# Half B's keys are transposed by DMA, and a chunk's decay weight sits on its values alone

## The chip, the cores and the metric

The kernel runs on all 8 cores of one Trainium2 chip. Each core computes one of the 8 prompt sequences and 16 of the 128 sample tokens; nothing passes between cores. The metric is device time in microseconds of the slowest core, as a median over runs.

## The reference, cut to what matters

Two layers, of which the second is a retention layer; each is followed by a SwiGLU block. Retention goes chunk by chunk (128 tokens), with a decay gamma per head:

```python
def ret_chunk(q, k, v, s0, log_g):
    scores = jnp.einsum('bihd,bjhd->bhij', q, k) * dmask          # dmask[i,j] = gamma^(i-j), i >= j
    o = jnp.einsum('bhij,bjhe->bihe', scores, v)
    o = o + jnp.einsum('bihd,bhde->bihe', q, s0) * cross          # cross[i] = gamma^(i+1)
    s_new = gamma^c * s0 + jnp.einsum('bjhd,bjhe->bhde', k * kdec, v)   # kdec[j] = gamma^(c-1-j)
# per head: o is normalised over its 512 values (GroupNorm), then silu(g) * on, then @ w_out
```

There are 4 heads with 256 key and 512 value channels. The sample group does one such step per token from a given state of 4 x 256 x 512 per sample, read from and written back to HBM.

## The kernel before

A sequence of 2048 tokens is worked as two halves, A (hA, with the 16 meta and 16 sample tokens) and B (hB). The order is: pooling and feed-forward of layer 0 for A, retention of A, then the feed-forward of A and the feed-forward of B, beside which the sample group's states stream through, then retention of B (`ret(1, ...)`), then the last feed-forward of B.

The program is recorded op by op. `Prog` finds the dependences and `Side` plans the order: generators such as `a_gen` and `b_gen` run beside the main line, and each `yield` hands a delay or an operation, whose planned end (`_clock`, line 159, a table of costs) says when the generator is resumed. Thus the order on each engine is fixed when the program is built, by planned times; on the chip each engine goes through its own queue in that order and waits on semaphores.

In retention, per head h: `qk_proj` makes keys K and queries q (rotated by DVE and POOL); `a_gen` makes for each chunk t the masked scores PMt (two matmuls into a bank, a DVE multiply by the causal mask) and, through a second PSUM bank, the transposed keys KD[:, t] (two TensorE transposes, `tr`, line 488, and a ScalarE copy). `v_proj` makes V with a decay weight per token (C_VS). `b_gen` then does for each chunk PMt x V, q x state copy (Sbf), and adds KD x V to the running state in psS; ScalarE copies psS to Sbf for the next chunk. `gate_gen` normalises (C_GE is its epsilon) and gates the output; `o_proj` follows one head behind. Everything in psS is kept relative to a decay reference: before, each chunk's key copy is scaled by gamma^(-128 t) and each state copy by gamma^(128 (t+1)).

There are five or six PSUM banks for all this (`ring['b']`); `room(k)` waits in the plan until k of them are not held. KD and PMt have one buffer for all heads, so chunk t of head h waits for chunk t of head h - 1 to be used (`prog['b', h - 1]`).

DMAs go by two queues, each in order: SP's (`load` and `store`, line 520: states, outputs) and POOL's (weights). A DMA's waits stand on the issuing queue, so what follows on that queue waits too.

The lines that matter below: 481 `mm`, 489 `tr`, 498 `act`, 502 `acopy`, 505 `tt`, 514 `stto` (the sample group's state update on DVE), 202 the DMA issue.

## Time and profile before

| | us |
|---|---|
| median of 3 runs (1679.96 to 2389.19) | 1682.67 |
| the profiled execution, device time | 1678.12 |
| its span on the slowest core (core 3) | 1676.6 |
| spans of the cores | 1658.4 to 1676.6 |

| engine, slowest core | busy us | share of the span |
|---|---|---|
| PE (TensorE matmul) | 1606.3 | 96% |
| DVE | 756.1 | 45% |
| ACT | 689.9 | 41% |
| POOL | 337.2 | 20% |

The span runs from the first to the last instruction; the device time of the execution has 1.5 us around it. A busy PE is not a PE at its peak: matmuls overlap, so what one costs is read from the distance of starts, not from its duration. PEclk is the clock that TensorE was granted, 1.00 for 2.4 GHz and 0.50 for 1.2 GHz. On core 3 the stages lie as follows: start and layer 0 of A to about 335 us, retention of A to 620, sample group beside the feed-forward of A and B to 1155, retention of B to 1430, last feed-forward to 1676.

### The profile page before, as it was taken

To read this page: it belongs to the slowest core of one execution; us is meant where nothing else is said; L and a number is where in the kernel's file an instruction comes from. 1 tells how busy PE (TensorE), PEld (TensorE's weight loads), DVE (VectorE), ACT (ScalarE), POOL (GpSimd) and SP (SyncE) were. 2 spreads that over 40 slices of the span, in tenths; PEclk is the share of its full clock that TensorE was granted. 3 is DMA by queue.
4 is the path that set the end of the run, shared out by engine and by line. 5 is a ranking of instruction groups with operands and counts; after the bars stand their busy time and mean duration, and the time that the engine had idled before them with its cause. 6 is when DMAs were issued, how large, how long until landed. Compare 5 with 4: busy or idle time off the path is not lost.

```text
span 1676.6 us, 28802 instructions; the slowest of 8 cores (1658.4 to 1676.6 us)
## 1 busy us (share of the span) xinstructions
PE 1606.3 (96%) x10076; PEld 920.0 (55%) x10076; DVE 756.1 (45%) x1455; ACT 689.9 (41%) x1279; POOL 337.2 (20%) x560
## 2 busy tenths in 40 slices
PE   5999999999999999997999988999999998999997
PEld 3666666655555564443454433456545555666665
DVE  4432222643736563452363623355546648323225
ACT  3311012257555635545544414444565566110122
POOL 5110000343524311110010000013514232001000
PEclk9899999999999999998999999999999999999998
DMA  9157966787776788799988998676434313213433
GB/s 235 25 114 164 181 138 129 130 143 145 154 134 119 155 225 251 228 246 232 213 191 247 238 246 274 225 192 136 90 78 81 59 39 107 66 48 102 68 53 103
DMA packets 78892, 251.68 MB, mean 150 GB/s; under 512 B 8896, under 2 KB 15360, under 8 KB 78736
## 3 DMA queue, kind: packets, MB, share of 16 engines
q0 software_dynamic: 32656, 114.57, 38.3%
q1 hardware_dynamic: 46096, 135.27, 26.3%
q8 instruction: 85, 1.39, 0.3%
q14 instruction: 55, 0.45, 0.1%
HBM read 254.79 MB, written 73.27 MB: 196 GB/s over the span
## 4 chain that ended last, share of the span: by engine, by line
PE 82%; DMA 9%; DVE 3%; issue 2%; ACT 1%; SPq 1%; POOL 1%; DVEq 0%; POOLq 0%; ACTq 0%
PE pm L481 69%; PE psU L481 6%; DMA nrs<-fb 5%; PE psS L481 5%; DMA fb<-sret 2%; DMA nrs<-cs_sb 2%; PE pm L489 1%; SPq L202 1%; DVE xn L514 1%; DMA fb<-xtok 1%; PE pm L485 0%; DVE hB L505 0%; ACT on L498 0%; DVE stt L979 0%; DVE fb L514 0%
## 5 line engine op out<-in xcount | busy, mean ns | idle before, releaser
L481 PE MATMUL pm<-xn,w 128*128 128x512 bf16 (+7 forms) x4424 | 794.2, 338 | 13.3 <-DVE hB L505 5.7
L481 PEld LDWEIGHTS pm<-xn,w 128*128 128x128 bf16 x4424 | 432.6, 99 | 341.1 <-issue 33.4
L481 PE MATMUL pm<-U,w 128*128 128x512 bf16 (+6 forms) x2290 | 405.8, 334 | 3.7 <-DVE hA L505 2.6
L481 PEld LDWEIGHTS pm<-U,w 128*128 128x128 bf16 x2290 | 222.0, 98 | 168.3 <-issue 13.3
L505 DVE TENSOR_TENSOR U<-pm,rot 128x512 bf16<-128x512 f32 (+5 forms) x206 | 121.2, 588 | 367.7 <-PE pm L481 356.2
L498 ACT ACTIVATE rot<-pm 128x512 bf16<-128x512 f32 (+6 forms) x190 | 98.7, 519 | 370.5 <-PE pm L481 370.4
L505 DVE TENSOR_TENSOR hB<-pm,hB 128x347 f32<-128x347 f32 (+4 forms) x164 | 85.0, 539 | 86.7 <-PE pm L481 85.6
L481 PE MATMUL pm<-w,xn 128*128 128x512 bf16 (+1 forms) x488 | 113.3, 379 | 1.7 <-DVE U L505 1.7
L505 DVE TENSOR_TENSOR hA<-pm,hA 128x512 f32<-128x512 f32 (+4 forms) x131 | 76.0, 597 | 73.8 <-PE pm L481 73.2
L505 POOL TENSOR_TENSOR U<-rot 128x352 bf16<-128x352 f32 (+2 forms) x96 | 95.4, 1014 | 55.8 <-DVE rot L505 55.7
L498 ACT ACTIVATE af<-pm,cf_sb 128x128 f32<-128x128 bf16 x232 | 87.2, 462 | 24.0 <-DVE U L505 15.2
L505 DVE TENSOR_TENSOR rot<-pm,cs_sb 128x352 f32<-128x352 f32 (+2 forms) x168 | 78.5, 512 | 26.9 <-PE pm L481 14.3
L665 POOL TENSOR_TENSOR stt<-stt,cf_sb 128x1 f32<-128x1 f32 x65 | 36.3, 558 | 233.5 <-DVE stt L509 233.4
L498 ACT ACTIVATE Sbf<-psS 128x1024 bf16<-128x1024 f32 x56 | 57.4, 1025 | 56.1 <-PE psS L481 55.9
L498 ACT ACTIVATE U<-pm 128x256 bf16<-128x256 bf16 (+7 forms) x127 | 54.8, 451 | 60.3 <-PE pm L481 59.8
L481 PEld LDWEIGHTS pm<-w,xn 128*128 128x128 bf16 (+1 forms) x488 | 45.8, 98 | 54.3 <-issue 4.8
L498 ACT ACTIVATE U<-pm,cf_sb 128x512 bf16<-128x512 f32 (+1 forms) x77 | 52.6, 690 | 52.3 <-PE pm L481 52.0
L514 DVE SCALAR_TENSOR_TENSOR fb<-fb,psS 128x1024 f32<-128x1024 f32 x41 | 49.8, 1214 | 46.1 <-DMA fb<-sret 28.3
L202 POOL DMA_DIRECT2D w<-c_gu x49 | 27.6, 565 | 200.9 <-PE pm L481 197.9
L505 DVE TENSOR_TENSOR U<-af,U 128x512 bf16<-128x512 f32 x64 | 55.4, 866 | 23.2 <-ACT af L498 23.2
L498 ACT ACTIVATE xn<-hB 128x347 bf16<-128x347 f32 (+4 forms) x68 | 33.4, 508 | 59.9 <-DVE hB L505 59.5
L505 DVE TENSOR_TENSOR U<-pm,cb_sb 128x128 bf16<-128x128 f32 x54 | 15.6, 291 | 91.6 <-PE pm L489 70.9
(254 smaller groups left out, 1509.3 us busy)
## 6 DMA issues: line engine op xcount, KB each, us to landing
w<-c_gu POOLq DMA_DIRECT2D x49, 512.0 KB, 7.7
fb<-sret SPq DMA_DIRECT2D x41, 512.0 KB, 8.5
nrs<-fb SPq DMA_DIRECT2D x41, 512.0 KB, 8.4
w<-w_gu POOLq DMA_DIRECT2D x39, 512.0 KB, 9.3
w<-w_d POOLq DMA_DIRECT2D x32, 352.0 KB, 6.1
w<-c_d POOLq DMA_DIRECT2D x32, 352.0 KB, 5.1
c_gu<-w SPq DMA_DIRECT2D x17, 512.0 KB, 7.9
w<-w_qk POOLq DMA_DIRECT2D x16, 512.0 KB, 9.7
```

The source lines that it names most:

```text
L202: h.dma_start(out=o_ap, in_=i_ap).then_inc(s, 16)
L481: return P.op('pe', lambda h: h.matmul(out, lhsT=lhsT, rhs=rhs, start=start, stop=stop, skip_group_check=skip), ins=[lhsT, rhs], outs=[out ...
L489: return P.op('pe', lambda h: h.transpose(out, in_, idn), ins=[in_, idn], outs=[out], cost=0.056)
L498: return P.op('act', lambda h: h.activation(out=out, in_=in_, func=func, scale=scale, **kw), ins=ins, outs=[out] + ([accum] if accum is no ...
L505: return P.op(eng, lambda h: h.tensor_tensor(out=out, in0=a, in1=b, op=op), ins=[a, b], outs=[out])
L514: return P.op('dve', lambda h: h.scalar_tensor_tensor(out=out, in0=a, scalar=s, in1=b, op0=op0, op1=op1), ins=ins, outs=[out])
L665: return P.op('pool', lambda h: h.tensor_tensor(out=dst, in0=dst, in1=cf[0:n, C_NH:C_NH + k], op=ALU.pow), ins=[dst, cf[0:n, C_NH:C_NH + k ...
```

## The change

In half B the keys are transposed by 16 DMAs on SP's queue (`dma_start_transpose`, SBUF to SBUF, four chunks and one half of the key channels each, at t = 0 and t = 4 of every head) in place of 64 TensorE transposes, their bank and 32 ScalarE copies. For t = 0 and 4 the generator waits in the plan until four chunks of the previous head are used. Since a DMA cannot scale, the decay of the chunk goes into the values' weights: C_VS and C_GE get a column for each chunk, and in both halves the copies to KD and Sbf carry no scale. `b_gen` asks for 3 free banks in place of 4 and yields once more, `yield kdt[h, t]`, which in half B holds the transposing DMA and in half A None.

```diff
+        def xpose_dma(out, in_, sem):
+            return P.dma('sp', [(out, in_)], ins=[in_], outs=[out], sem=sem, transpose=True)
...
             for t in range(8):
-                while h and prog['b', h - 1] < t + 1:
-                    yield 0.3
+                if hf == 0:
+                    while h and prog['b', h - 1] < t + 1:
+                        yield 0.3
+                elif t % 4 == 0:
+                    while h and prog['b', h - 1] < t + 4:
+                        yield 0.3
+                    for c in range(2):
+                        xt = xpose_dma(KD[:, t:t + 4, c * 128:(c + 1) * 128], K[:, c, t * 128:t * 128 + 512], ('tk', c, t))
...
-                pt = bank()
-                ptb = pt[:].bitcast(BF16)[:, 0:256]
-                for c in range(2):
-                    tr(ptb[:, c * 128:(c + 1) * 128], K[:, c, cc], ident)
+                if hf == 0:
+                    pt = bank()
+                    ptb = pt[:].bitcast(BF16)[:, 0:256]
+                    for c in range(2):
+                        tr(ptb[:, c * 128:(c + 1) * 128], K[:, c, cc], ident)
                 tt(PMt[:, t, :], ps[:, 0:128], causal, ALU.mult)
                 held.remove(ps)
-                act(KD[:, t, :], ptb, ACT.Copy, scale=float(gam[h] ** (-128.0 * t)))
+                if hf == 0:
+                    acopy(KD[:, t, :], ptb)
                 prog['a', h] = t + 1
+                kdt[h, t] = xt if hf else None
...
-                yield from room(4)
+                yield kdt[h, t]
+                yield from room(3)
...
-                    xs = act(Sbf[(t + 1) % 2][:], psS[:], ACT.Copy, scale=float(gam[h] ** (128.0 * (t + 1))))
+                    xs = acopy(Sbf[(t + 1) % 2][:], psS[:])
...
-                sc = C_V8 if t == 8 else C_VS
-                act(V[0:n, t, :], pb[0:n, :], ACT.Copy, scale=cf[0:n, sc + h:sc + h + 1])
+                sc = (C_V8 if t == 8 else C_VS + 4 * t) + h
+                act(V[0:n, t, :], pb[0:n, :], ACT.Copy, scale=cf[0:n, sc:sc + 1])
...
-        cf[:, C_VS + h] = np.exp(-(j + 1.0) * lg[h])
+        for t in range(8):
+            cf[:, C_VS + 4 * t + h] = np.exp(-(128.0 * t + j + 1.0) * lg[h])
+            cf[:, C_GE + 4 * t + h] = EPS * 256.0 * np.exp(-2.0 * (128.0 * t + j + 1.0) * lg[h])
```

What stands on TensorE's queue at the start of head 0's value projection in half B (L481 `pm<-w,xn` is a value tile, `pm<-U` 128x128 a score, L489 `cb_sb,U` the key transposes, then the first chunk of `b_gen`), before:

```order
L481 MATMUL pm<-w,xn 128x512 x8
L481 MATMUL pm<-U 128x128 x2
L489 MATMUL pm<-cb_sb,U 128x128 x2
L481 MATMUL pm<-w,xn 128x512 x8
L481 MATMUL pm<-U 128x128 x2
L489 MATMUL pm<-cb_sb,U 128x128 x2
L481 MATMUL pm<-w,xn 128x512 x8
L481 MATMUL pm<-U 128x128 x2
L489 MATMUL pm<-cb_sb,U 128x128 x2
L481 MATMUL pm<-U 128x512
L481 MATMUL pm<-Sbf,U 128x512 x2
L481 MATMUL psS<-U 128x512 x2
```

and of the change, at the same place:

```order
L481 MATMUL pm<-w,xn 128x512 x8
L481 MATMUL pm<-U 128x128 x2
L481 MATMUL pm<-w,xn 128x512 x8
L481 MATMUL pm<-U 128x128 x2
L481 MATMUL pm<-w,xn 128x512 x8
L481 MATMUL pm<-U 128x128 x2
L481 MATMUL pm<-w,xn 128x512 x8
L481 MATMUL pm<-U 128x128 x2
L481 MATMUL pm<-U 128x512
L481 MATMUL pm<-Sbf,U 128x512 x2
L481 MATMUL psS<-U 128x512 x2
```

The transposes are gone, and the first chunk of `b_gen` stands behind four value tiles, before behind three.

The end of SP's queue, from the sample group's last states on (`nrs` stores and `sret` loads are the sample group's, `sscr` is half A's state of a head, `nrp` the final state of a head), before:

```order
L202 DMA hA<-sret 128x1024
L202 DMA hA<-sscr 128x1024
L202 DMA nrs<-hA 128x1024
L202 DMA hA<-sret 128x1024
L202 DMA nrs<-hA 128x1024
L202 DMA hA<-sscr 128x1024
L202 DMA nrs<-hA 128x1024 x2
L202 DMA nrp<-fb 128x1024
L202 DMA hA<-sscr 128x1024
```

and of the change:

```order
L202 DMA nrs<-hA 128x1024
L202 DMA_TRANSPOSE U<-U 128x4x128 x2
L202 DMA hA<-sscr 128x1024
L202 DMA nrs<-hA 128x1024
L202 DMA_TRANSPOSE U<-U 128x4x128 x2
L202 DMA nrs<-hA 128x1024
L202 DMA_TRANSPOSE U<-U 128x4x128 x2
L202 DMA nrp<-fb 128x1024
L202 DMA_TRANSPOSE U<-U 128x4x128 x2
L202 DMA hA<-sscr 128x1024
L202 DMA nrp<-fb 128x1024
L202 DMA_TRANSPOSE U<-U 128x4x128 x4
```

Head 0's first pair stands behind the third-last state store, its second behind the second-last; from head 2 on the pairs of t = 0 and t = 4 stand together behind the previous head's state store.

On TensorE, between the last chunk of head 2 (its psS row is the first here) and the first of head 3, the change has:

```order
L481 MATMUL psS<-U 128x512 x2
L481 MATMUL pm<-w,xn 128x512 x16
L489 MATMUL pm<-cb_sb,on 128x128 x4
L481 MATMUL pm<-w,xn 128x512 x8
L481 MATMUL pm<-U 128x128 x2
L481 MATMUL pm<-w,xn 128x512 x8
L481 MATMUL pm<-U 128x128 x2
L481 MATMUL pm<-xn,w 128x512 x8
L481 MATMUL pm<-U 128x128 x2
L481 MATMUL pm<-xn,w 128x512 x8
L481 MATMUL pm<-U 128x128 x2
L481 MATMUL pm<-xn,w 128x512 x8
```

After these come one more score and the three operations of head 3's first chunk. Between the same two places of heads 1 and 2 stand ten groups of eight, eight scores and two sets of four `on` transposes, and between head 1's first score and its first chunk thirteen groups of eight, eight scores and three chunks of head 0.

## Rows read from the trace of the kernel before

**Rows 1.** The page: engines, and the chain that ended last by engine and line

```profile
PE 1606.3 (96%) x10076; PEld 920.0 (55%) x10076; DVE 756.1 (45%) x1455; ACT 689.9 (41%) x1279; POOL 337.2 (20%) x560
...
PE 82%; DMA 9%; DVE 3%; issue 2%; ACT 1%; SPq 1%; POOL 1%; DVEq 0%; POOLq 0%; ACTq 0%
PE pm L481 69%; PE psU L481 6%; DMA nrs<-fb 5%; PE psS L481 5%; DMA fb<-sret 2%; DMA nrs<-cs_sb 2%; PE pm L489 1%; SPq L202 1%; DVE xn L514 1%; DMA fb<-xtok 1%; PE pm L485 0%; DVE hB L505 0%; ACT on L498 0%; DVE stt L979 0%; DVE fb L514 0%
```

**Rows 2.** The list of cores: span and mean granted clock of TensorE

```profile
core 0: 1659.9 us, clock 0.984
...
core 3: 1676.6 us, clock 0.979
```

**Rows 3.** Windows, core 3: stretch, length, busy of PE, PEld, DVE, ACT, POOL, clock, DMA

```profile
335.00:620.00 285.00, 281.00 (x1775) 158.05 (x1773) 155.90 (x339) 169.37 (x340) 102.51 (x173) 0.99 0.77 151
...
790.00:1155.00 365.00, 353.37 (x1970) 172.65 (x1967) 168.75 (x260) 154.87 (x240) 45.47 (x70) 0.97 0.85 222
1158.00:1424.00 266.00, 253.42 (x1614) 141.74 (x1612) 155.47 (x349) 164.60 (x317) 84.70 (x143) 1.00 0.37 80
```

**Rows 4.** Windows, the same 50 us on core 3 and then on core 0

```profile
970.00:1020.00 50.00, 40.95 (x169) 16.49 (x167) 16.30 (x23) 13.50 (x20) 3.70 (x7) 0.86 0.98 249
...
970.00:1020.00 50.00, 49.74 (x238) 22.19 (x242) 18.95 (x26) 19.30 (x29) 4.24 (x8) 1.00 0.91 285
```

**Rows 5.** Timeline of DVE: start, length, operation, in brackets idle before it

```profile
1001.28 1.22 DVE L514 SCALAR_TENSOR_TENSOR fb<-fb,psS 128x1024 f32<-128x1024 f32 x1 [9.94 <-DMA fb<-sret]
```

**Rows 6.** TensorE's waits, 1155 to 1435 us: in total, times, longest

```profile
PE pm L481 <- ACT on L498: 3.4, 7, 0.9
PE pm L481 <- DVE U L505: 3.1, 8, 0.7
...
PE pm L489 <- ACT U L498: 0.4, 1, 0.4
...
PE pm L489 <- ACT af L498: 0.2, 1, 0.2
```

**Rows 7.** Groups by form, 1155 to 1435 us: count, busy us, mean ns, idle before

```profile
L498 ACT ACTIVATE Sbf<-psS 128x1024 bf16<-128x1024 f32 x28 | 28.7, 1024 | 31.6 <-PE psS L481 31.3
...
L498 ACT ACTIVATE U<-pm 128x256 bf16<-128x256 bf16 x29 | 11.2, 386 | 0.0
...
L489 PE MATMUL pm<-cb_sb,U 128*128 128x128 bf16 x58 | 8.0, 219 | 0.6 <-ACT U L498 0.4 <-ACT af L498 0.2
```

**Rows 8.** Timeline of TensorE at the start of head 0's value projection in half B

```profile
1158.70 1.89 PE L481 MATMUL pm<-w,xn 128*128 128x512 bf16 x8
1160.43 0.28 PE L481 MATMUL pm<-U 128*128 128x128 bf16 x2
1160.54 0.28 PE L489 MATMUL pm<-cb_sb,U 128*128 128x128 bf16 x2
1160.65 1.89 PE L481 MATMUL pm<-w,xn 128*128 128x512 bf16 x8
```

**Rows 9.** DMA issues: the table of constants, count, KB each, us to landing

```profile
cf_sb<-cf SPq DMA_DIRECT2D x1, 114.5 KB, 5.3
```

**Rows 10.** DMA issues of SP, whole span and (last two) 1100 to 1435 us

```profile
yTa<-hA SPq DMA_DIRECT2D x16, 170.5 KB, 17.8
...
nps_x<-U SPq DMA_DIRECT2D x1, 64.0 KB, 2.0
...
hA<-sscr SPq DMA_DIRECT2D x4, 512.0 KB, 5.0
nrp<-fb SPq DMA_DIRECT2D x4, 512.0 KB, 2.7
```

**Rows 11.** Timeline of SP's queue: start, length of the issue

```profile
1154.69 0.34 SPq L202 DMA_DIRECT2D nrs<-hA  x1
...
1344.44 0.33 SPq L202 DMA_DIRECT2D nrp<-fb  x1
```

**Rows 12.** Timeline of TensorE: the last state matmuls of head 2 in half B

```profile
1342.60 0.59 PE L481 MATMUL psS<-U 128*128 128x512 bf16 x2
```

More of the change, by code:

```diff
@@ L191, in op, with dma @@
         return self._mk(eng, fn, ins, outs, cost=cost)
-    def dma(self, eng, pairs, ins=(), outs=(), sem=None, is_out=False):
+    def dma(self, eng, pairs, ins=(), outs=(), sem=None, is_out=False, transpose=False):
         ent = self.dma_sems.get(sem)
@@ L201, in fn @@
             for (o_ap, i_ap) in pairs:
-                h.dma_start(out=o_ap, in_=i_ap).then_inc(s, 16)
+                (h.dma_start_transpose if transpose else h.dma_start)(out=o_ap, in_=i_ap).then_inc(s, 16)
             return None
```

6 lines of the change are left out of this document (3 added, 3 removed).

## The prediction

> **What bounds the kernel now.** I began with the page and the list of cores. TensorE is busy for 96% of the span of the slowest core, and the chain that ended last is TensorE for 82% of it, by far the most of that on line 481, the matmuls [rows 1]. So what shortens TensorE's queue shortens the time, and what only lightens another engine does not. The list of cores shows a second thing: core 3 needs 1676.6 us and core 0, with the same program, 1659.9 [rows 2]; 16.7 us of the result come from something that is not the same on all cores.
>
> The windows by stage say where that is [rows 3]. Half B's retention (1158 to 1424 us on core 3) has TensorE busy for 253.42 of 266 us at a granted clock of 1.00, the full 2.4 GHz, with the DMA engines at a share of 0.37. The stage before it, in which the sample group's states stream through (790 to 1155), has DMA at 0.85. Inside it, from 970 to 1020 us, core 3 has TensorE busy for 40.95 us at a clock of 0.86, core 0 for 49.74 at 1.00 [rows 4]. What core 3 waits for is seen on VectorE: a state update stands idle for 9.94 us until a state load lands [rows 5], and the adds into hB, whose banks TensorE wants next, stand behind it in the queue.
>
> In half B's retention TensorE is idle for no more than 12.6 us (266 less 253.42), and the list of its waits spreads them over many short ones, ACT on and DVE U ahead [rows 6]. There is little to win beyond the work itself.
>
> **The change part by part.** *TensorE, removed.* Half B has 64 transposes of keys (4 heads, 8 chunks, 2 each); the row of the 58 that go into pm gives each 219 ns [rows 7], but that is a duration from start to modelled end, and matmuls overlap. The timeline has the right price: the pair of transposes starts at 1160.54 and the next matmuls at 1160.65, so a pair takes 0.11 us of the queue, and eight matmuls of 512 columns take from 1158.70 to 1160.43, 1.73 us [rows 8]. 32 pairs by 0.11 are 3.6 us, all on the path.
>
> Here the Trainium skill would mislead: "VectorE: DVE Perf Modes", section "The three transpose paths", gives 390 ns for a 128x128 bf16 transpose on TensorE. By it the 64 would be worth 25 us; the trace disagrees (55 ns each), and the measurement decides.
>
> *ScalarE, removed.* 32 copies of keys out of PSUM by 386 ns [rows 7] are 12.4 us. ScalarE is busy for 164.60 of 266 us there [rows 3], so this is worth nothing directly. But the transposes themselves wait 0.6 us (0.4 and 0.2) for a bank, and projections wait 3.1 us, in eight pieces, on DVE U: the mask after a score, whose bank the next projection takes [rows 6]. Without the transposes' bank there is one more to rotate through. Between nothing and 7.1 us of the waits (0.6, 3.1 and the 3.4 on ACT on) can go; I take 0.6 and half of 3.1, 2.1 us, since the gate chain behind ACT on stays as it is.
>
> *Other scales.* The state copy (1024 ns [rows 7]) and half A's key copy lose a constant scale and keep their shapes; whatever that changes lies on ScalarE, which has 101 us free in this stage. Nothing. The decay table grows by 56 columns to 285, from 114.5 to 142.5 KB; its load lands in 5.3 us at the kernel's start [rows 9], where TensorE has no cover. 28 KB more are 1.3 us if all of the 5.3 were transfer, and 0.15 at the rate of the 512 KB that land in 2.7 us [rows 10]; I take 0.2, since a load that small mostly queues.
>
> *SP, added.* 16 DMA transposes of 128 KB from SBUF to SBUF, in pairs (c = 0, 1). No row shows one. The nearest below is a store of 64 KB in 2.0 us and one of 512 KB in 2.7; in this stage an SBUF load of 512 KB takes 5.0; the slowest of like size is a yTa store of 170.5 KB, 17.8 us, under the sample traffic [rows 10]. So a pair lands between 2.7 and 17.8 us after its issue. I take 10, two of the 5.0 in line, because one queue serves both and the stage has less than half the DMA share of the one with the yTa stores [rows 3].
>
> What covers it is what TensorE does between issue and the first psS matmul of the chunk that needs the keys. Counted from the order rows by the prices above (1.73 for eight of 512 columns, 0.11 for a pair of 128, 0.22 for one of 512): head 0, four value tiles, four scores and three matmuls, 8.0 us from the first value tile; SP stands free 4.0 us sooner, at 1154.69 against 1158.70, when the third-last state store has gone out [rows 8, 11], so 8 to 12 us. Head 1 has about 28 us, head 2 19.3 less the 1.6 explained next, 17.7. Head 3 has 13.5, less 1.6, because SP first issues the store of head 2's state, at 1344.44 (and 0.33 of issuing) after the last state matmuls, 1342.60 plus 0.59 [rows 11, 12]: 11.9. With 10 us only head 0 can be late, by 0 to 2; I take 1.0. Behind the waiting psS matmul stands all of TensorE's queue, so a lateness counts in full. Second pairs (t = 4) are needed four chunks later, some 33 us (32 chunks in 266), and stay covered. On SP, behind the transposes, stand only the load of the next head's state and a state store, which nothing needs soon. If a weight load is slowed: weights come by POOL's queue, and none of TensorE's waits in this stage is for a weight load; the longest in sum are those of [rows 6].
>
> By the same section of the skill's page the DMA crossbar takes 1309 ns for 128x128, so a pair, eight blocks, would take 10.5 us, head 0 would be up to 2.5 us late, and the sum would move by about 1.5. The page's table of rules says to use TensorE where the result may go to PSUM; no run here shows a transpose by DMA yet.
>
> *The planner, both halves.* b_gen now asks for three free banks where it asked for four and yields once more, so half A's order moves too, and with it the start of the sample group. Half A's retention has 281.00 of 285 us busy [rows 3]; what can be won there is under 4 us, and I take nothing.
>
> **The sum.** -3.6 (transposes) -2.1 (waits) +0.2 (table) +1.0 (head 0 late) = -4.5 us. The profiled execution took 1678.12 us, its span 1676.6 and 1.5 around it, so it would take 1673.6. The median of the runs shown, 1682.67, lies 4.55 above it; set against that, 1678.2.
>
> **The rivals.** *Transposes land late* (slower). The price follows from the four covers: with landing L the loss is the sum of L-10, L-28, L-17.7 and L-11.9 where positive. At 17.8 us that is 7.8 + 0.1 + 5.9 = 13.8; with the -5.5 of the rest, 1691.0. It passes the other side (no gain) at L of about 14, and 2% slower, 1716.3, at about 27. For it: the transposes are issued just when two weight buffers come free and are refilled, on the same 16 engines. Against it: DMA at 0.37. 0.17, of which 0.04 beyond 2%.
>
> *The sample stage moves.* The order of state loads, yTa stores and hB adds is planned anew, since half A's timing shifts. If three quarters of core 3's 16.7 us go, 12.5, the time is 1682.67 - 4.5 - 12.5 = 1665.7; 0.14. If the updates come to stand worse, by another 9 us (the 50 us window's difference of 49.74 and 40.95), it is 1687; 0.11. For it: VectorE's queue is in order and 9.94 us of waiting is one load. Against: bytes and pacing are the same.
>
> *The freed time comes back as a wait* in half B's retention, because a head's chain from psS through the state copy and back bounds it; then only the 0.6 of bank waits goes and the time is 1682. For it: the chain runs through three engines. Against it: a chunk's copy is 1.02 us [rows 7], and the 32 chunks share 266 us, 8.3 each. 0.03.
>
> **How the numbers follow.** The forecast, 1672 to 1684 around 1678.2, has 0.55. To hold 8 in 10 the range must reach into the late transposes and into the sample stage's both signs: 1664 to 1692 leaves out the late cases beyond L of 18 (about 0.08) and the luckiest sample stage (0.04). Since cases of both signs hold much of the chance, the forecast's own range is the 1672 to 1684. About 2% is what a measurement of this kernel can tell from no change: below 1649.0 nothing that I priced leads, 0.01; above 1716.3 only transposes slower than any row, 0.04; within, 0.95.
>
> **What would show it.** Right: 64 fewer rows of transposes of U in half B's retention, the stage from the first value tile to its end 4 to 6 us shorter on every core, DVE U waits about halved, pairs landing within 10 us, at most one short wait of psS on a DMA, in head 0. Wrong: psS waiting on the transposes in heads 2 and 3; granted clock below 1.00 inside the stage; or a total that moves while the stage does not, with the difference between cores 0 and 3 changed, which would be the sample stage.

## The result, and the profile after

| | us |
|---|---|
| before, median of 4 runs | 1681.32 |
| after, median of 4 runs | 1656.51 |
| ratio, with its 95% interval | 0.9863 [0.9821, 0.9905] |
| profiled execution after, device time | 1657.12 |
| its span on the slowest core (core 7) | 1655.6 |
| spans of the cores after | 1635.2 to 1655.6 |

The time is below the range of the prediction (1664 to 1692), and the gain is 1.4%, inside the 2% that it called no change. Now and then an execution of either kernel has all cores of a die at a lower clock for its whole length; ratios and means below leave those out, while medians of times hold every execution.

The page of the kernel after: the span, the engines, the DMA packets, and the chain that ended last by engine and line.

```profile
span 1655.6 us, 28592 instructions; the slowest of 8 cores (1635.2 to 1655.6 us)
...
PE 1606.1 (97%) x10012; PEld 918.9 (56%) x10012; DVE 752.4 (45%) x1455; ACT 680.2 (41%) x1247; POOL 334.5 (20%) x560
...
DMA packets 87450, 253.79 MB, mean 153 GB/s; under 512 B 17584, under 2 KB 24048, under 8 KB 87296
...
PE 93%; DVE 3%; issue 1%; DMA 1%; ACT 1%; POOL 1%; DVEq 0%; POOLq 0%; SPq 0%; ACTq 0%
```

TensorE has 64 matmuls fewer, as it should, but its busy time on the slowest core is the same as in [rows 1] (1606.1 against 1606.3), and the span is 21.0 us shorter. The chain was TensorE for 82% with 9% DMA, all but a little of that state loads and stores; here it is TensorE for 93% with 1% DMA. That difference is not the gain, though. The same kernel in another execution (e3 below), faster by 8 us, has

```profile
PE 83%; DMA 10%; DVE 3%; issue 2%; ACT 1%; SPq 1%; POOL 0%; DVEq 0%; POOLq 0%; ACTq 0%
```

so the chain of one slowest core says which core came last and by what way, not what the change was worth.

The sample stage on the slowest core, first before (core 3), then after (core 7), and half B's retention on core 3 after (stretch, length, busy of PE, PEld, DVE, ACT, POOL, clock, DMA share, GB/s):

```profile
580.00:1158.00 578.00, 555.29 (x3118) 275.75 (x3117) 273.35 (x426) 257.38 (x416) 75.97 (x126) 0.97 0.86 226
582.00:1147.00 565.00, 558.35 (x3126) 277.97 (x3125) 274.99 (x428) 257.79 (x413) 77.16 (x129) 0.97 0.85 233
1124.00:1356.00 232.00, 226.48 (x1355) 122.89 (x1353) 130.29 (x298) 138.77 (x250) 79.76 (x134) 0.99 0.46 91
```

From slowest core to slowest core the stage is 13 us shorter, and TensorE's idle time in it falls from 22.7 to 6.7 us. In half B's retention core 3 is idle for 5.5 of 232 us, where it was for 12.6 of 266 [rows 3]. Core 3, the slowest core before, is here the fastest, but which core is slow differs from one execution to the next, and the cores lie as far apart after (20.4 us) as before (18.2). Cores 4 to 7 after have lost time to something else, told at the end under "A third clock": some 10 us each in this stage, 5 as a mean over all cores, which neither the execution before nor e3 has.

To set all runs side by side I cut every core's timeline at the same marks: half A's retention (first to last use of psS by it), the sample stage (from there to the first value tile of half B), and half B (from there to the last matmul). The numbers are means over the eight cores of the profiled execution, worked out from the timelines, and the waits are the lists of waits of the sample stage, summed and averaged alike. "Mean span" is the mean over all cores and all executions that enter the ratio, less the same mean of the kernel before on the same chip (1667.2, 1668.0, 1664.2, 1664.7 and 1665.5 us; 1665.2 in the profiled execution for the second row). The mean span of a single execution scatters by about 3 us (standard deviation) and by up to 13 between extremes, so the column's differences are good to some 3 us, and to 4 for e2, e8, e13, e14 and e17, which have three executions each; e10 has one. The stages come from one execution each, for e1, e2, e16 and e18 among the longest of theirs and for e3, e4 and e12 the shortest.

How far a single execution can be trusted is seen in this: up to half B, VectorE, POOL and SP's queue of the change, e2, e3, e5, e7, e8, e15 and e17 go through one order, and those of the kernel before and e1 through another (ScalarE's copies differ in their scale alone). The sample stages of the first eight are 554.0 to 565.9 us, 558.0 in the mean; those of the other two 566.3 and 573.7.

| kernel | median us | ratio to before | mean span | half A | sample stage | half B | TensorE waits in the sample stage, of these for VectorE | VectorE waits for state loads |
|---|---|---|---|---|---|---|---|---|
| before | 1681.32 | 1 | 0 | 236.4 | 566.3 | 510.9 | 14.7, 11.1 | 20.2 |
| after | 1656.51 | 0.9863 | -19 | 235.4 | 558.5 | 500.7 | 6.4, 0.7 | 9.5 |
| e3, the change again | 1662.63 | 0.9869 | -20.8 | 235.4 | 554.0 | 500.6 | 6.5, 0.3 | 16.5 |
| e1, half A's order kept | 1673.76 | 0.9963 | -9.9 | 236.4 | 573.7 | 502.1 | 20.7, 15.5 | 28.2 |
| e2, half B on TensorE | 1669.45 | 0.9898 | -13.3 | 235.3 | 565.9 | 505.6 | 14.1, 1.5 | 24.0 |
| e5, one turn in half A alone | 1670.48 | 0.9914 | -11.9 | 235.3 | 560.2 | 510.1 | 8.2, 1.3 | 15.0 |
| e6, two turns in half A | 1671.58 | 0.9951 | -5.9 | 242.5 | 559.5 | 510.6 | 12.1, 6.0 | 10.1 |
| e4, both halves by DMA | 1677.23 | 0.9978 | -3.6 | 253.6 | 554.9 | 503.3 | 7.9, 1.7 | 18.5 |
| e7, each transpose twice | 1675.24 | 0.9984 | -2.5 | 235.3 | 558.5 | 519.9 | 6.7, 0.3 | 14.4 |
| e8, one transpose a chunk | 1657.08 | 0.9854 | -20.9 | 235.4 | 556.3 | 503.5 | 5.8, 0.3 | 10.9 |
| e9, before, lead 6 | 1664.26 | 0.9937 | -10.7 | 236.4 | 552.9 | 510.9 | 6.0, 3.5 | 13.1 |
| e10, before, lead 9 | 1706.83 | none | -2.7 (one execution) | 236.4 | 559.2 | 515.0 | 10.3, 6.5 | 19.8 |
| e11, change, lead 6 | 1672.42 | 0.9990 | -5.8 | 235.3 | 557.9 | 512.7 | 9.3, 0.4 | 12.9 |
| e12, change, lead 9 | 1674.40 | 1.0011 | -12.4 | 235.3 | 553.6 | 509.6 | 7.0, 1.7 | 8.3 |
| e13, before, quarter loads | 1659.26 | 0.9888 | -10.9 | 236.4 | 553.9 | 510.9 | 5.9, 5.7 | 4.8 |
| e14, change, quarter loads | 1644.76 | 0.9790 | -27.0 | 235.4 | 549.6 | 500.7 | 3.5, 0 | 3.5 |
| e15, transposes on ACT's queue | 1671.38 | 0.9952 | -6.0 | 235.3 | 554.3 | 518.2 | 7.4, 1.8 | 13.1 |
| e16, lead 9, ACT's queue | 1678.16 | 1.0000 | +1.1 | 235.3 | 561.6 | 521.0 | 12.6, 4.1 | 15.3 |
| e17, head 0 on TensorE | 1655.92 | 0.9897 | -21.9 | 235.3 | 556.2 | 502.2 | 8.1, 0.8 | 16.6 |
| e18, head 0 on TensorE, lead 9 | 1661.92 | 0.9889 | -19.8 | 235.3 | 558.2 | 505.6 | 10.1, 2.8 | 9.9 |

### The profile page after: what moved, and what is told of

Read it like the earlier page. It is cut to its first block, busy times and chain, and to the rows that moved or that the text cites. A ratio compares the mean times of both kernels' runs of the same rounds, so it can differ in the third digit from the quotient of the medians.

```text
span 1655.6 us, 28592 instructions; the slowest of 8 cores (1635.2 to 1655.6 us)
## 1 busy us (share of the span) xinstructions
PE 1606.1 (97%) x10012; PEld 918.9 (56%) x10012; DVE 752.4 (45%) x1455; ACT 680.2 (41%) x1247; POOL 334.5 (20%) x560
## 4 chain that ended last, share of the span: by engine, by line
PE 93%; DVE 3%; issue 1%; DMA 1%; ACT 1%; POOL 1%; DVEq 0%; POOLq 0%; SPq 0%; ACTq 0%
PE pm L481 79%; PE psU L481 6%; PE psS L481 5%; PE pm L489 1%; DMA cs_sb<-xtok 1%; DVE xn L514 1%; PE pm L485 0%; DVE hB L505 0%; DMA cf_sb<-cf 0%; ACT on L498 0%; DVE stt L982 0%; DVE hA L505 0%; DVE hB L514 0%; PE psU L489 0%; POOL ssq L668 0%
## 5 line engine op out<-in xcount | busy, mean ns | idle before, releaser
L481 PE MATMUL pm<-xn,w 128*128 128x512 bf16 (+7 forms) x4472 | 805.2, 339 | 5.8 <-DVE xn L514 3.7
L481 PEld LDWEIGHTS pm<-xn,w 128*128 128x128 bf16 x4472 | 438.5, 99 | 339.4 <-issue 37.0
L481 PE MATMUL pm<-U,w 128*128 128x512 bf16 (+6 forms) x2274 | 408.5, 336 | 3.0 <-POOL stt L509 2.2
L481 PEld LDWEIGHTS pm<-U,w 128*128 128x128 bf16 x2274 | 221.9, 99 | 170.4 <-issue 23.9
L505 DVE TENSOR_TENSOR hB<-pm,hB 128x346 f32<-128x346 f32 (+4 forms) x163 | 85.6, 541 | 101.3 <-PE pm L481 100.1
L481 PE MATMUL pm<-w,xn 128*128 128x512 bf16 (+1 forms) x464 | 107.7, 379 | 0.0
L505 POOL TENSOR_TENSOR U<-rot 128x352 bf16<-128x352 f32 (+2 forms) x96 | 91.4, 972 | 64.5 <-DVE rot L505 64.5
L505 DVE TENSOR_TENSOR rot<-pm,cs_sb 128x352 f32<-128x352 f32 (+2 forms) x174 | 81.3, 512 | 34.2 <-PE pm L481 17.5
L502 ACT CAST Sbf<-psS 128x1024 bf16<-128x1024 f32 x60 | 61.2, 1019 | 68.4 <-PE psS L481 68.4
L481 PEld LDWEIGHTS pm<-w,xn 128*128 128x128 bf16 (+1 forms) x464 | 43.8, 98 | 48.9 <-issue 1.6
L498 ACT ACTIVATE U<-pm 128x512 bf16<-128x512 f32 (+6 forms) x76 | 38.7, 510 | 65.8 <-PE pm L481 65.2
L505 DVE TENSOR_TENSOR U<-af,U 128x512 bf16<-128x512 f32 x64 | 48.7, 761 | 36.8 <-ACT af L498 36.2
L498 ACT ACTIVATE rot<-psS 128x384 bf16<-128x384 f32 (+1 forms) x32 | 14.8, 464 | 100.2 <-PE psS L481 100.2
L202 POOL DMA_DIRECT2D w<-c_d x32 | 17.7, 552 | 189.8 <-PE pm L481 181.3
## 6 DMA issues: line engine op xcount, KB each, us to landing
w<-w_qk POOLq DMA_DIRECT2D x16, 512.0 KB, 10.7
```

Source lines behind the costliest of these rows:

```text
L202: (h.dma_start_transpose if transpose else h.dma_start)(out=o_ap, in_=i_ap).then_inc(s, 16)
L481: return P.op('pe', lambda h: h.matmul(out, lhsT=lhsT, rhs=rhs, start=start, stop=stop, skip_group_check=skip), ins=[lhsT, rhs], outs=[out ...
L498: return P.op('act', lambda h: h.activation(out=out, in_=in_, func=func, scale=scale, **kw), ins=ins, outs=[out] + ([accum] if accum is no ...
L502: return P.op('act', lambda h: h.copy(out=out, in_=in_), ins=[in_], outs=[out])
L505: return P.op(eng, lambda h: h.tensor_tensor(out=out, in0=a, in1=b, op=op), ins=[a, b], outs=[out])
```

## The experiments

**Which part of the change gives what: e1, e2, e3.** Three kernels tell the two halves of the change apart. e1 is the change with half A's generator as it was:

```diff
-                yield kdt[h, t]
-                yield from room(3)
+                if hf:
+                    yield kdt[h, t]
+                yield from room(3 if hf else 4)
```

> The change, but half A is planned as before (four free banks, no additional yield), so that the order of every engine up to half B's retention is that of the kernel before; half B transposes by DMA. Theory 1 (two gains: the retention of half B is shorter on every core, and the sample stage is shorter because its order is another): from the end of half A's retention to half B's, 563 to 582 us as before, half B's retention 228 to 230 us as in the change; 9 to 11 us faster than before, ratio about 0.994. Rival (all of the gain comes from half B, and the sample stage went better by chance of the chip): about as fast as the change, 0.986.

e2 is the change with half B's keys on TensorE, all else (scales, table, planner lines) kept; the three tests `if hf == 0:` in `a_gen` become `if True:`, and `kdt[h, t]` is None in both halves.

> The change, but half B too transposes its keys on TensorE; everything before half B stands in the order of the change. Theory 1: sample stage as in the change (552 to 570 us between the two retentions), half B's retention about 237 us as before; 11 to 15 us faster than before, ratio 0.991 to 0.993. Rival (the gain is half B's): no faster than before, 1.000. A second rival (three free banks in place of four shorten half B, not the DMA): half B's retention falls towards 230 us here too.

e3 is the change unaltered, on the same chip as the other two.

> The change itself beside the others on one chip: ratio 0.986 as measured (0.982 to 0.991), half B's retention 228 to 230 us. If the two parts add, its gain is the sum of the gains of the two kernels that hold one part each; if the sample stage went better by chance, it comes out between 0.990 and 0.995 here.

Measured: 0.9963 [0.9923, 1.0004], 0.9898 [0.9798, 0.9998] and 0.9869 [0.9794, 0.9944]. In mean span e1 gives 9.9 us, 8.8 of them in half B, and e2 13.3, with TensorE still doing the transposes. So most of the gain does not come from the DMAs. Half B alone goes from 510.9 us over 505.6 (e2) to 500.7 (the change): half of its gain comes without the DMAs too. The other scales are not the reason: the state copy takes 1016 ns in e2's half B where it took 1024 [rows 7], and the copy of the keys 378 where it took 386. What is left is the order that the planner lines make; the additional turn and the three banks were not run apart in half B.

**One extra turn: e5 and e6.** e5 is the kernel before with one line, and nothing of the DMAs, the scales or half B:

```diff
+                if hf == 0:
+                    yield None
                 yield from room(4)
```

> The kernel before with one added line: half A's loop over the chunks gives its turn once (yield None) before it asks for its four banks. Half B's order on TensorE is that of the kernel before, its keys are transposed on TensorE, scales and table are as before. Theory A (the order of half A and of the sample stage, made by the one extra turn, shortens the sample stage): sample stage 550 to 570 us on the cores (560 to 578 in the kernel before), half B's retention unchanged at 240.6 us, tail 270.6; in all 1671 to 1677, the kernel with half B on TensorE (1669.5) plus the 5 us that its half B was shorter. Rival B (the sample stage's length is chance of a run, or comes with the new scales): sample stage 560 to 578 us, in all 1679 to 1684.

e6 has that `yield None` twice.

> The kernel before with two added turns (yield None twice) in half A's loop alone: a third order of half A and of the sample stage that nobody chose, half B as before. Theory A1 (the order of the kernel before is an unlucky one, and most others are shorter): sample stage 550 to 570 us, in all 1670 to 1677. Theory A2 (orders scatter to both sides, the change happened on a short one): sample stage anywhere from 550 to 590 us, and 1681 or more is as likely as less. Rival B (the stage does not hang on the order): 560 to 578 us, in all 1679 to 1684.

Measured: 0.9914 [0.9872, 0.9956] and 0.9951 [0.9921, 0.9981]. One line that computes nothing gives 11.9 us of mean span. Half A has 1.1 of it and half B 0.8; the rest, some 10 us, must lie in the sample stage, where the one profiled execution (a long one, with the third clock on cores 4 to 7) shows 6.1. e1's 9.9 and e5's 11.9 make 21.8, and the change itself has 20.8 on the chip of e1: the two parts add. Of the theories on the order A1 is the nearer one: both other orders of the sample stage are shorter than the kernel before's. But e6 loses 6 us in half A's retention (242.5), which I had not expected.

What the turn does is seen in TensorE's waits of the sample stage (engine, tile, line, what it waited for: us in total, times, longest). The kernel before, core 3, 580 to 1158 us:

```profile
PE pm L481 <- DVE hB L505: 5.7, 3, 4.5
PE pm L481 <- DVE U L505: 5.4, 1, 5.4
PE psU L481 <- ACT Sbf L502: 3.4, 1, 3.4
PE pm L481 <- ACT U L498: 3.2, 3, 1.6
PE pm L481 <- DVE hA L505: 2.8, 3, 2.2
PE pm L481 <- DVE xn L514: 2.3, 2, 2.1
```

The same of e5 on core 2, 580 to 1134 us:

```profile
PE psU L481 <- ACT Sbf L502: 3.2, 1, 3.2
PE pm L489 <- POOL rs L665: 2.7, 1, 2.7
PE pm L481 <- ACT xn L498: 0.7, 3, 0.3
```

All waits for VectorE are gone on this core (on core 5 one of 8.1 us on hB is left). VectorE's own wait for state loads is not: as a mean over the cores it is 20.2 us before, 15.0 in e5, 24.0 in e2, and TensorE waits for VectorE 11.1, 1.3 and 1.5. So e2 shows that the new order does without sooner loads. What it changes is whether TensorE comes for the work that stands behind a waiting update. The kernel before, VectorE on core 3, with the product behind the waiting update (start, length, operation, in brackets the idle time before it):

```profile
783.85 1.22 DVE L514 SCALAR_TENSOR_TENSOR fb<-fb,psS 128x1024 f32<-128x1024 f32 x1 [9.32 <-DMA fb<-sret]
784.99 0.68 DVE L505 TENSOR_TENSOR U<-pm,rot 128x512 bf16<-128x512 f32 x1
```

and TensorE on the same core:

```profile
785.82 0.29 PE L481 MATMUL pm<-cb_sb,U 128*128 128x1 bf16 x5 [5.36 <-DVE U L505]
```

The product behind the update ends at 785.67, and TensorE, idle for 5.36 us, starts 0.15 us later. In the new order, VectorE and TensorE of e2, core 2:

```profile
788.84 1.22 DVE L514 SCALAR_TENSOR_TENSOR fb<-fb,psS 128x1024 f32<-128x1024 f32 x1 [6.79 <-DMA fb<-sret]
789.97 0.68 DVE L505 TENSOR_TENSOR U<-pm,rot 128x512 bf16<-128x512 f32 x1
```

```profile
780.65 17.65 PE L481 MATMUL pm<-xn,w 128*128 128x512 bf16 x80
```

An update waits as before, the same kind of product stands behind it, and TensorE is busy all the while. Not every wait goes: in e2 8.8 of TensorE's 14.1 us are for ScalarE's state copies (Sbf).

A wait also costs more than its length, because the granted clock falls behind it. TensorE before, core 3, and the window around it:

```profile
1013.14 3.57 PE L481 MATMUL pm<-xn,w 128*128 128x512 bf16 x8 [4.45 <-DVE hB L505]
```

```profile
1012.00:1018.50 6.50, 5.09 (x12) 1.61 (x13) 3.40 (x5) 4.53 (x7) 0.53 (x1) 0.50 0.88 245
```

After 4.45 us of waiting the clock is 0.50 (1.2 GHz), and eight matmuls of 512 columns take 3.57 us in place of 1.89 [rows 8]. On the traces of the clock such stretches cost 11.1 us of the sample stage before (580 to 1130 us, mean over the cores) and 4.3 both in the change and in e3.

**Are the loads the root: e13 and e14.** Both kernels with every engine's order kept to the instruction, and each load of a sample state a quarter as large (256 of 1024 columns; three quarters of every state are not loaded).

```diff
-                    loads[u] = load(where[u][0], sret[u // 4, u % 4], where[u][1])
+                    loads[u] = P.dma('sp', [(where[u][0], sret[u // 4, u % 4])], outs=[where[u][0]], sem=where[u][1], part=256)
```

> The kernel before, every engine's order unchanged, but each load of a sample state brings a quarter of its columns (128 KB instead of 512), so that it lands sooner; the sample group's output is left wrong by that, all other work is done. Theory A (the root is VectorE waiting for state loads, with TensorE's adds and masks behind it): TensorE's wait for VectorE in the sample stage falls from 11.1 to under 3 us (mean of the cores), the stage from 566 to 550 to 556 us, in all 1662 to 1670. Rival B (the order costs by banks and engines, loads or no loads): TensorE's wait for VectorE stays above 7 us, the stage above 560, in all 1673 or more.

> The change, every engine's order unchanged, with state loads of a quarter as in the run on the kernel before (the sample group's output is left wrong in the same way). Theory A: TensorE hardly waits for VectorE in the change as it is, so the stage shortens only by what else the traffic costs, from 556 to 549 to 554 us, in all 1646 to 1655; the sample stage of the two kernels differs by under 4 us where it differed by 11. Rival B: the stage stays 8 us or more shorter than that of the kernel before with quarter loads, in all 10 us beyond what half B gives.

Measured: 0.9888 [0.9801, 0.9976] and 0.9790 [0.9722, 0.9858]. With sooner loads the kernel before loses 12.4 us of its sample stage (566.3 to 553.9) and the change 4.4 to 8.9 (from 554.0 and 558.5 to 549.6): the two stages, 7.8 to 12.3 us apart, are 4.3 apart (of the two orders' means above, 570.0 and 558.0, 12.0). The loads are the root of most of the difference. Whether it is their landing sooner or the traffic that they no longer make is not separated: both are smaller here. Of my numbers, a difference under 4 us was just missed, and TensorE's wait for VectorE under 3 us clearly, with 5.7 in e13. What is left is in the waits of e13, core 0, 580 to 1133 us:

```profile
PE pm L481 <- DVE hA L505: 2.8, 3, 2.3
PE pm L481 <- DVE xn L514: 2.3, 2, 2.1
```

and of e14, core 0, 580 to 1130 us:

```profile
PE pm L489 <- POOL rs L668: 2.7, 1, 2.7
PE pm L481 <- ACT xn L498: 0.7, 3, 0.3
```

The waits on hA and xn in the kernel before stand in its order, loads or no loads: 5.1 us, against 3.4 of other waits in the change.

**A longer lead for the updates: e9 to e12.** If an update waits because it stands too early, planning it later should help. One constant of the plan, in the kernel before (e9, e10) and in the change (e11, e12):

```diff
-                    while handoff or out[0] < b or not past(loads[u], 3.0):
+                    while handoff or out[0] < b or not past(loads[u], 6.0):
```

> The kernel before with one constant changed: the planner places a sample state's update on VectorE no sooner than 6 us, instead of 3, after its load is planned to have landed. Half A's and half B's order stay. In the kernel before TensorE waits for VectorE 11.1 us (mean of the cores) in the sample stage, and VectorE 20.2 us for state loads. Theory A (an update that stands too early in VectorE's queue waits for its load, and the adds and masks behind it hold TensorE up): with 3 us more of lead VectorE's wait for loads falls below 10 us, TensorE's wait for VectorE below 5, the sample stage from a mean of 566 to about 558 us, in all 1669 to 1675. Rival B (the stage is bound by the stream of states on the DMA queues, whose share is 0.85, and a later update only holds its buffer longer): the loads come later too, TensorE's waits stay above 10 us, in all 1679 to 1690. Rival C (only which work stands behind the waiting update counts, not how long it waits): VectorE's wait falls, but TensorE's wait for it is anything from 1 to 12 us.

> As the run with a lead of 6 us, with 9. Theory A: VectorE's wait for loads under 3 us, TensorE's wait for VectorE under 3, sample stage 550 to 560 us, in all 1666 to 1673. Rival B: buffers are held 6 us longer than before, the stream of states slows and the sample stage is 570 us or more, in all 1685 or more. Rival C: VectorE's wait is gone, TensorE's wait for it anything from 1 to 12 us.

> The change with a lead of 6 us. In the change TensorE waits for VectorE 0.3 to 0.7 us in the sample stage (mean of the cores), though VectorE waits 9.5 to 16.5 us for state loads. Theory A: nothing left to win on VectorE, the sample stage stays at a mean of 554 to 559 us, in all 1652 to 1662. Rival B: buffers held longer, sample stage 562 us or more, in all 1665 or more. Rival C (the change's order is a lucky one, and any re-planning loses it): TensorE waits for VectorE 4 us or more, in all 1662 to 1670.

> The change with a lead of 9 us. Theory A: in all 1650 to 1662, TensorE's wait for VectorE under 2 us. Rival B: buffers held 6 us longer, sample stage 565 us or more, in all 1668 or more. Rival C: TensorE waits for VectorE 4 us or more, in all 1662 to 1670.

Measured: 0.9937 [0.9902, 0.9973] for e9, 0.9990 [0.9964, 1.0017] for e11 and 1.0011 [0.9986, 1.0036] for e12. e10 has no ratio, since only one of its four executions (1668.95 us) can be compared; its median counts for nothing. e9 gains 10.7 us of mean span with half A and half B as they were, as Theory A has it, but hardly for its reason: VectorE's wait for loads is 13.1 where it was 20.2, not below 10, and with 9 us of lead 19.8; and executions of one order scatter from 9.5 to 24.0 in it. So no run shows that the longer lead shortens that wait. TensorE's wait for VectorE (11.1, 3.5 and 6.5 us with leads of 3, 6 and 9) fits Rival C, whose 1 to 12 us could hardly miss; the lead changes VectorE's order as well, and the two were not separated. Of the sample stage I can say what a given order costs; why this order and not that one is the good one is not settled further than this.

e11 and e12 show something else. Their sample stages are like the change's, but half B takes 512.7 and 509.6 us in place of 500.7. Here the transposes are late. TensorE of e11, core 4:

```profile
1151.08 0.58 PE L481 MATMUL psS<-U 128*128 128x512 bf16 x1 [6.83 <-DMA U<-U]
1158.34 0.58 PE L481 MATMUL psS<-U 128*128 128x512 bf16 x1 [6.68 <-DMA U<-U]
```

SP's queue of e12, core 7 (start, length of the issue):

```profile
1135.36 2.79 SPq L202 DMA_TRANSPOSE U<-U  x2
1140.01 8.81 SPq L202 DMA_DIRECT2D nrs<-hA  x1
1148.92 25.28 SPq L202 DMA_DIRECT2D hA<-sret  x2
```

and POOL of the same core:

```profile
1163.82 0.91 POOL L505 TENSOR_TENSOR U<-rot 128x341 bf16<-128x341 f32 x1 [11.09 <-DMA U<-U]
1168.59 0.90 POOL L505 TENSOR_TENSOR U<-rot 128x341 bf16<-128x341 f32 x1 [3.86 <-DMA U<-U]
```

The pair issued at 1135.36 holds its source until 1163.8 and 1168.6, 28 and 33 us later. It is head 0's second pair, which I had called covered for 33 us, as its result is. But K, which it reads, is wanted sooner: the rotation of head 1's keys writes K, waits on POOL, and TensorE then waits 12.2 us for DVE rot. That consumer I had not counted.

**What the covers bear: e4, e7, e8.** e4 lets half A's keys go by DMA as well, in the place of the three tests on hf.

> The change with half A's 64 key transposes by DMA as well (the 8 of the meta tokens stay). By the price of half B (3.6 us of transposes and up to 5 of waits): half A's retention 4 to 6 us shorter, since half A had only 4 us of waits; the sample stage is planned anew once more and may go either way, so 0.980 to 0.990. Rival (transposes compete with half A's copies of weights to HBM on the same queue and land late): half A's retention longer than 235 us.

Measured: 0.9978 [0.9942, 1.0013]. Half A's retention goes from 235.4 to 253.6 us and eats the gain. TensorE's waits there, core 7, 330 to 630 us, first line:

```profile
PE psS L481 <- DMA U<-U: 16.1, 2, 10.5
```

and SP's queue at its start:

```profile
340.92 3.06 SPq L202 DMA_TRANSPOSE U<-U  x2
...
344.65 11.85 SPq L202 DMA_TRANSPOSE U<-U  x2
```

The rival of this run is right: the same DMAs cost 18 us here. So "transposes land late" is true here, where the DMA engines are busier. The windows from the issue of a first pair to its landing, core 7 of the change (head 0 of half B), of e4 (half A), and of e15 below (columns as above; a packet counts where it starts, so a share can pass 1):

```profile
1143.70:1150.50 6.80, 6.80 (x43) 3.95 (x42) 2.44 (x4) 5.08 (x9) 4.20 (x7) 1.00 0.63 139
340.90:358.60 17.70, 7.20 (x39) 3.12 (x38) 1.17 (x4) 3.71 (x5) 0.00 (x0) 0.80 1.06 169
1145.50:1162.20 16.70, 6.30 (x36) 2.88 (x33) 4.47 (x7) 5.64 (x9) 0.37 (x1) 0.77 1.01 229
```

The pair of the change lands in 6.7 us at a DMA share of 0.63; at shares of about 1 the others take some 17 us. e7 issues each of half B's 16 twice:

```diff
-                        xt = xpose_dma(KD[:, t:t + 4, c * 128:(c + 1) * 128], K[:, c, t * 128:t * 128 + 512], ('tk', c, t))
+                        for _ in range(2):
+                            xt = xpose_dma(KD[:, t:t + 4, c * 128:(c + 1) * 128], K[:, c, t * 128:t * 128 + 512], ('tk', c, t))
```

> The change, with each of its 16 transposing DMAs issued twice, 32 in all; the work that TensorE has to wait for is doubled, its own work is that of the change. Theory A (the covers of the prediction hold: 10, 28, 17.7 and 11.9 us for the four heads, and the loss is the sum of landing less cover): the pairs of the change land in about 8 us and are not waited for; doubled they take about 16 us, head 0 is late by 6 and head 3 by 4 us, half B's retention 241 to 243 us instead of 231 to 233, in all 1665 to 1673. Rival B (the covers are longer than worked out, so nothing is late): retention 231 to 234 us, in all 1655 to 1663. Rival C (the second reading holds K's buffer longer, and the next head's rotation waits for it, with the projections behind): retention 245 us or more, with waits on DVE rot or POOL in the list of TensorE's waits rather than on the DMA.

Measured: 0.9984 [0.9957, 1.0010], half B 19.2 us longer than in the change. TensorE of core 5:

```profile
1169.83 0.58 PE L481 MATMUL psS<-U 128*128 128x512 bf16 x1 [7.64 <-DMA U<-U]
...
1295.19 0.38 PE L481 MATMUL psS<-U 128*128 128x512 bf16 x1 [1.33 <-DMA U<-U]
1298.16 0.38 PE L481 MATMUL psS<-U 128*128 128x512 bf16 x1 [2.59 <-DMA U<-U]
```

7.6 us in head 0 and 3.9 in head 2, where I had written 6 in head 0 and 4 in head 3. Head 3, with the shorter cover, waits for nothing on this core, and the agreement in size is luck: the plan moved with the doubled DMAs, head 0's four went out at 1142.04 and the last was there 27.8 us later, and TensorE came for them at 1162.2, not 8 to 12 us after the issue. Much of the other 8 us goes with the clock (0.88 from 1150 to 1200 on this core, where the change has 1.00). e8 cuts the work into 64 DMAs of 32 KB, one for each chunk and c, each planned as soon as its one chunk of the previous head is used.

> The change with one transposing DMA of 32 KB for each chunk and each c, 64 in place of 16 of 128 KB. Theory A (the landing is mostly transfer, and what TensorE needs first is one chunk): the first chunk's keys land in 3 to 5 us, nothing is late, half B's retention 231 to 233 us as in the change, in all 1653 to 1661. Rival B (each transposing DMA has a fixed cost on SP and in its queue, so four times as many take longer in sum): SP is busy issuing for 64 times 1.2 us or more, later chunks of heads 0 and 3 land late, retention 236 us or more, in all 1661 to 1675.

Measured: 0.9854 [0.9813, 0.9895], the time of the change; half B is 503.5 us, 2.8 longer. The time is Theory A's, the retention (235.3 as a mean) lies between the theories. The size of the pieces matters little.

**Another queue, and head 0 by itself: e15 to e18.** e15 issues the transposes from ScalarE (`P.dma('act', ...)` in `xpose_dma`), TensorE's order unchanged; e16 is that with the lead of 9.

> The change with its 16 transposing DMAs issued by ScalarE in place of SP; TensorE's order is kept to the instruction. Theory A (where they stand behind or between state stores and loads on SP's queue sets the landing): head 0's pairs no longer share a queue with the sample group's last stores and loads, no wait on them in half B's retention, but ScalarE is held 1.2 to 8 us at each issue, 16 times, and what TensorE wants from it is late: retention 232 to 240 us, in all 1655 to 1665. Rival B (the landing is set by the 16 DMA engines, whatever the queue, and ScalarE's issues are cheap): retention 231 to 233 us, in all 1654 to 1660.

> The change with a lead of 9 us for the state updates and the transposes issued by ScalarE. With SP's queue this order had the shortest mean span but on four cores a retention of 243 to 250 us, through a second pair that took up to 30 us behind the sample group's last loads and stores. Theory A (SP's queue is the cause): no core above 238 us, mean span under 1648, in all 1650 to 1662. Rival B (the 16 DMA engines are the cause, whatever the queue): still cores above 243 us, in all 1668 or more.

Measured: 0.9952 [0.9914, 0.9991] and 1.0000 [0.9957, 1.0043], half B 518.2 and 521.0 us. ScalarE and TensorE of e15, core 7:

```profile
1145.57 2.93 ACTq L202 DMA_TRANSPOSE U<-U  x2
```

```profile
1162.14 1.01 PE L481 MATMUL psS<-U 128*128 128x512 bf16 x2 [10.40 <-DMA U<-U]
```

The first value tile starts at 1143.6 on this core. In ScalarE's queue the pair goes out 2.0 us after it, in SP's of the kernel after 3.6 us before, and alone on its queue it still needs 16.6 us to land. Both theories on e15 missed. SP's queue is not the cause of the landing, as Rival B of both runs has it (in e16 every core is above 250 us), but ScalarE's issues come 5.6 us later to begin with, and the landing is 10 us longer than the change's. That the DMA engines are the cause is argued from the shares above; no run empties them. e17 and e18 keep head 0's keys on TensorE (`if hf == 0 or h == 0:`), e18 with the lead of 9.

> The change, with head 0's keys of half B transposed on TensorE as before and those of heads 1 to 3 by DMA. In the change nothing is late in most executions, so nothing is won; 16 transposes come back, 8 pairs of 0.11 us, 0.9 us, and perhaps some of the bank waits. Theory A (only TensorE's own work counts): retention 232 to 235 us on every core, in all 1655 to 1664. Rival B (the order is planned anew from head 0 on, and loses the waits gained): 236 us or more, 1664 or more.

> The same with a lead of 9 us for the state updates. With all heads by DMA this order had retentions of 235 to 250 us, the longer ones through head 0's second pair, for which the rotation of the next head's keys waited. Theory A (head 0 alone carries the loss): retention 233 to 237 us on every core, sample stage 549 to 563 us, in all 1648 to 1660, the shortest of all. Rival B (the transposes of the next heads, or the traffic of the last states itself, keep it long): cores above 243 us, in all 1665 or more.

Measured: 0.9897 [0.9862, 0.9933] and 0.9889 [0.9848, 0.9930]; in mean span -21.9 and -19.8. e17 is the change again, with 1.5 us more in half B, as Theory A has it. In e18 half B is 505.6 us where e12 had 509.6: retention is 234.5 to 236.3 on six cores and 240.1 and 242.8 on two, so head 0 carried most of the loss, not all. No version beats the change beyond what a run can tell.

## Why the prediction was wrong

**The planner, "I take nothing": the step that failed.** I held half A's retention, where 4 us could be won, to be what an extra turn can touch, and it did give 1.0. The turn's larger effect is on what is planned after it. I had a shorter sample stage as a rival, with a chance of 0.14 and a price of 12.5 us, and a shorter sample stage is what came: -11.9 us of mean span in e5, with a single line. That the sizes agree is luck. The price was three quarters of core 3's excess over core 0, and that excess did not go: the cores are 20.4 us apart after, 18.2 before, and the mean of all of them fell. A hint stands in [rows 1], which I read for TensorE's 82% alone: 9% of the chain, some 150 us, was state loads and stores, so the order of that stage could lie on the path (e3 has 10%, so the share does not say how much). The turn and the three banks in half B were priced at nothing as well and gave 4.5 us (510.1 in e5 to 505.6 in e2).

**Transposes off TensorE, -3.6, and waits, -2.1: right.** From e2 to the change half B goes from 505.6 to 500.7 us, by 4.9; the forecast for the DMA part, with 1.0 of lateness and 0.2 for the table, was 4.5. (The table's 0.2 is less than these runs can tell.) The waits of half B's retention after, core 3, 1124 to 1360 us:

```profile
PE pm L481 <- POOL stt L509: 2.2, 1, 2.2
PE pm L481 <- ACT on L498: 1.4, 3, 0.8
PE pm L481 <- DVE hB L505: 0.7, 2, 0.4
...
```

DVE U, 3.1 us in [rows 6], is gone altogether, and ACT on is down from 3.4 there to 1.4. But a part of that is the order's: TensorE's waits in half B's retention sum to 10.8 us on core 3 before (1158 to 1400 us), to 7.3 in e2, which keeps the transposes, and to 5.3 here (the list's smaller ones are 1.0 together). So 2.0 us go with the DMAs, the 2.1 forecast, and 3.5 with the order, which had no term.

**Head 0's pair late by 1.0: nothing was late.** TensorE waits for no transpose in half B. SP's queue after, core 7, and TensorE when it comes to the first chunk:

```profile
1143.68 2.65 SPq L202 DMA_TRANSPOSE U<-U  x2
...
1153.09 6.32 SPq L202 DMA_TRANSPOSE U<-U  x2
```

```profile
1147.31 1.89 PE L481 MATMUL pm<-w,xn 128*128 128x512 bf16 x8
...
1155.31 0.59 PE L481 MATMUL psS<-U 128*128 128x512 bf16 x2
```

The cover is 8.0 us from the first value tile and 11.6 from the issue, as worked out (8 to 12), and the pair lands in 6.7. One landing of 10 us for every pair was the weak figure: in the change a single DMA takes 2.4 to 15.6 us on this core, longest in head 0's second pair and in head 2. The covers of heads 2 and 3 are 17.5 and 11.7 us there, as worked out (17.7 and 11.9). The margin is thin: e1, with half B's order of the change, has two cores of eight with retentions of 245.8 and 237.0 us (231.0 on the best). On the first, head 2's pairs took 14.79 us to issue, TensorE waited 2.2 us for them, and 8.3 us for a rotation held up as in e12. By the Trainium skill, "VectorE: DVE Perf Modes", section "The three transpose paths", a pair was an estimate of 10.5 us; the measured first pairs lie on both sides of it, 6.7 us in the change and 16.6 in e15.

**The rivals.** "Transposes land late" was priced by four covers of KD's readers; the runs show it real in half A (e4), with leads of 6 and 9 and on ScalarE's queue, and that K's next writer belongs to the list. "Freed time returns as wait" fell. The gain is inside the 2% as forecast; the range missed it because its lower end, 1664, was that rival's 1665.7 and no more, while the shorter stage came together with half B's order, which had no price.

## What to carry to other kernels

Where a planner sets the order, a changed yield or bank count is a change of the whole order behind it: look up where the stages behind it wait for transfers through an in-order queue, and test the line alone before crediting the operations that came with it. An update that waits for a load costs what stands behind it in its queue, if the bottleneck comes for that work meanwhile, and a wait of TensorE costs the clock after it besides. Judge an order by several executions: single ones of one order lay 12 us apart here. A transpose by DMA paid in half B, where it landed before TensorE came for it, and not in half A, where TensorE waited 16.1 us for it in e4; count the next writer of its source as well as the reader of its result.

## What the runs showed of the hardware

**The transposing DMA.** One of 128 KB from SBUF to SBUF keeps SP 1.18 us at least, where a plain DMA takes 0.33, and up to 7.9 in the change and 11.85 for two in e4. The kernel has 8,688 packets under 512 B more than before for its 2 MB, some 240 B each (in e15, where they have a queue to themselves, it shows 8704 packets and 2.10 MB). The DMA issues of the kernel after, core 7, 1100 to 1400 us (count, median us to landing):

```profile
U<-U SPq DMA_TRANSPOSE x16, 7.2
```

It lands in 7.2 us there, and in 15 to 32 us in e4, e11, e12 and e15, where TensorE or POOL waits for it beside state or weight traffic.

**A third clock.** Windows of core 7 after, inside the sample stage (columns as above):

```profile
980.00:984.00 4.00, 4.00 (x20) 1.79 (x19) 0.82 (x2) 0.00 (x0) 0.00 (x0) 0.99 0.98 299
984.00:991.00 7.00, 7.00 (x28) 2.94 (x27) 2.65 (x4) 0.00 (x0) 1.06 (x2) 0.81 0.84 278
991.00:996.00 5.00, 5.00 (x25) 2.22 (x24) 2.93 (x4) 3.01 (x4) 0.53 (x1) 0.98 0.70 200
```

The granted clock is 0.81 for 7 us, neither 1.00 (2.4 GHz) nor 0.50 (1.2 GHz), while TensorE was busy without a gap before, during and after. Core 7 has eleven such stretches in the sample stage, and cores 4 to 7 have mean clocks of 0.977 to 0.981 against 0.983 to 0.988 on cores 0 to 3; in e3, the same program, no such difference is seen. Of the other runs e5 to e8, all on one chip, have 7 to 12 such stretches in this stage on each of cores 4 to 7 and none on cores 0 to 3, and e1 to e4 and e9 to e18, on three other chips, have none on any core. On the chip of e5 to e8 the kernel before has mean clocks of 0.980 on cores 4 to 7 and 0.983 on the others, over 16 executions. So the stretches go with the chip and the die, not with the change. The Trainium skill, "TensorE: Matmul & The Clock Gate", section "Seeing it yourself", states a limit of 13/16 of 2.4 GHz that a whole die can be put to; 13/16 is 0.8125, and the row agrees. No wait of TensorE stands at this stretch; what causes it, no run here can tell.
